# Group norm after a chunked scan: whole at the end, or chunk by chunk between the scan's own products

## The reference

```python
_, y = lax.scan(step, s0, (tm(rf), tm(decay), tm(kf), tm(vf), tm(kk), tm(af)))
y = tm(y)
mean = jnp.mean(y, axis=-1, keepdims=True)
var = jnp.mean(jnp.square(y - mean), axis=-1, keepdims=True)
y = ((y - mean) * lax.rsqrt(var + GN_EPS)).reshape(B, S, D) * ln_g + ln_b
bonus = jnp.sum(rf * kf * r_k, axis=-1, keepdims=True) * vf
out = (y + bonus.reshape(B, S, D)) * g.astype(jnp.float32)
return out.astype(h.dtype) @ w_o
...
sh1, sc1, gt1, sh2, sc2, gt2 = jnp.split(jax.nn.silu(c) @ ada_w[layer] + ada_b[layer], 6, axis=-1)
```

## Time and profile before

| | us |
|---|---|
| median of 3 runs (975.66 to 986.0) | 978.39 |
| the profiled execution | 980.12 |
| its span, first to last instruction | 978.3 |
| last matrix addition of the scan ends | 306.65 |
| first product of the output projection | 354.0 |
| PE / DVE / ACT / POOL busy | 856.2 / 660.2 / 418.4 / 112.1 |

### The profile page before, as it was taken

One profiled execution on the slowest core, in us unless ns is written; L12 is line 12 of the kernel. 1 busy time (PEld: TensorE's weight loads), 2 busy tenths in 40 slices (PEclk: granted clock), 3 DMA queues, 4 the chain that ended last, 5 costly groups with the idle time before them and its releaser, 6 DMA issues.

```text
span 978.3 us, 17529 instructions
## 1 busy us (share of the span) xinstructions
PE 856.2 (88%) x7477; PEld 733.1 (75%) x7477; DVE 660.2 (67%) x710; ACT 418.4 (43%) x585; POOL 112.1 (11%) x175
## 2 busy tenths in 40 slices
PE   1599997678888888999999999997777899999997
PEld 1597886567776455999999878995445689999976
DVE  4897965557557375999999957365675468545553
ACT  3279222333433146444343355514664653344441
POOL 8400002232331030000000003200000000000000
PEclk9799899799999689999999999996898999999999
DMA  8922335232205307799999556742000538655551
GB/s 322 338 89 85 100 116 197 76 118 88 89 13 189 129 20 258 259 372 368 368 370 384 201 172 208 213 140 77 1 1 1 173 129 278 238 175 194 192 172 43
DMA packets 71837, 170.16 MB, mean 174 GB/s; under 512 B 5432, under 2 KB 6736, under 8 KB 71760
## 3 DMA queue, kind: packets, MB, share of 16 engines
...
## 4 chain that ended last, share of the span: by engine, by line
PE 52%; DVE 34%; ACT 7%; issue 3%; DMA 2%; POOL 1%; ACTq 0%; DVEq 0%; POOLq 0%
DVE wlo L1025 8%; PE ps L1694 5%; PE ps L1698 5%; PE ps L1696 5%; PE ps L1683 5%; PE ps L1686 5%; PE ps L1685 5%; DVE acc L1269 5%; DVE acc L965 3%; PE ps L1620 2%; DVE gt L965 2%; PE ps L1512 2%; PE ps L1514 2%; PE ps L1515 2%; ACT whi L612 2%
## 5 line engine op out<-in xcount | busy, mean ns | idle before, releaser
L1025 DVE TENSOR_TENSOR wlo<-raw,whi 128x2048 fp32r<-128x2048 f32 x94 | 215.5, 2292 | 68.8 <-ACT whi L612 66.8
L612 ACT ACTIVATE whi<-raw 128x2048 fp32r<-128x2048 f32 x94 | 179.2, 1912 | 134.0 <-DMA raw<-in_mlp_down_dram 90.9
L1683 PE MATMUL ps<-ghi,whi 128*128 128x256 f32 x576 | 163.6, 284 | 2.5 <-DVE wlo L1025 1.4
L1686 PE MATMUL ps<-ghi,wlo 128*128 128x256 f32 x576 | 163.0, 283 | 0.0
L1685 PE MATMUL ps<-glo,whi 128*128 128x256 f32 x576 | 163.0, 283 | 0.0
L1683 PEld LDWEIGHTS ps<-ghi,whi 128*128 128x128 f32 x576 | 110.5, 192 | 5.1 <-issue 4.6
L1685 PEld LDWEIGHTS ps<-glo,whi 128*128 128x128 f32 x576 | 110.5, 192 | 0.7 <-issue 0.2
L1686 PEld LDWEIGHTS ps<-ghi,wlo 128*128 128x128 f32 x576 | 110.5, 192 | 0.0
L1694 PE MATMUL ps<-whi,hidhi 128*128 128x512 f32 x256 | 100.9, 394 | 2.4 <-DVE wlo L1025 2.4
L1696 PE MATMUL ps<-whi,hidlo 128*128 128x512 f32 x256 | 99.7, 390 | 0.0
L1698 PE MATMUL ps<-wlo,hidhi 128*128 128x512 f32 x256 | 99.6, 389 | 0.0
(11 more groups left out here) (337 smaller groups left out, 1637.7 us busy)
## 6 DMA issues: line engine op xcount, KB each, us to landing
raw<-in_mlp_up_dram SPq DMA_DIRECT2D x32, 1024.0 KB, 5.7
raw<-in_mlp_down_dram SPq DMA_DIRECT2D x32, 1024.0 KB, 5.2
raw<-in_ada_w_dram SPq DMA_DIRECT2D x24, 1024.0 KB, 6.1
late<-in_ada_w_dram SPq DMA_DIRECT2D x24, 1024.0 KB, 9.6
late<-in_kv_ada_w_dram SPq DMA_DIRECT2D x8, 1024.0 KB, 8.3
raw<-in_kv_w_dram SPq DMA_DIRECT2D x6, 1024.0 KB, 5.3
raw<-in_rw_k_dram SPq DMA_DIRECT2D x4, 1024.0 KB, 9.2
raw<-in_rw_r_dram SPq DMA_DIRECT2D x4, 1024.0 KB, 5.1
```

The costliest lines, as they stand in the source:

```text
L612: sc.activation(whi[i][:, :, :], raw[i][:, :].rearrange("p (k n) -> p k n", k=4), ACT.Copy).then_inc(s_hi, 1)
L1025: st.tell(dv.tensor_tensor(wlo[i][:, :, :], raw[i][:, :].rearrange("p (k n) -> p k n", k=4), whi[i][:, :, :].bitcast(F32), ALU.subtract), ...
L1683: mm(out_, whi[b][:, k, cols], hi[:, k0 + k, :], start=(first and k == 0 and m % 2 == 0), stop=False, skip_group_check=True)
L1686: ins = mm(out_, wlo[b][:, k, cols], hi[:, k0 + k, :], start=False, stop=False, skip_group_check=True)
```

## The change

The group norm is taken apart into entries of the scan's list, for 64 tokens each: `bonus` (spread the bonus sums, then on DVE times v, plus the norm's bias, times the gate, in place in `vF`), `centre` (one product with the matrix `centre`, identity minus head mean, gives the centred y; ACT squares it, DVE multiplies it by the gate times the norm's scale, `glng`), `variance` (head sums, root, reciprocal), `spread` (reciprocals back over features; DVE multiplies and adds), `high` and `low` (the split into `zhi`, `zlo`). Chunk c-1's stand inside chunk c. The list's ten places per chunk (after each `z` and each `p` pair) now hold several entries each, and `w`, `u`, `s`, `y`, `prep`, `turn`, `values` stand at other places. The four `rw_o` pieces are split in the last chunk (`piece_high`, `piece_low`). Behind the scan token block 0 of the projection is made in eight half pieces (`project`, 6 products each) between the last chunk's `u`, `y` and its norm; `out_projection` then makes token block 1 only. Modulation pieces 20 to 23 leave the place behind the scan: one stands behind the K/V pieces in the stream, three behind the query pieces, DVE does them there, and their column product is made on PE in the attention loop at unit 5. ACT makes `glng` ahead of the scan. `keep_clock(9)` goes.

```diff
+ADA_UNTIL = (6, 9, ADA_PIECES, ADA_PIECES)
...
-        between = [(x, c - 1, 0) for x in "wusy"] if c else []
...
+        slots = [[] for _ in range(10)]
+        if c == 0:
+            slots[0] = [("bonus", 0, 0)]
+            slots[7] = [("w", 0, 0)]
+        else:
+            slots[0] = [("u", before, 0)]
+            slots[1] = [("s", before, 0)]
+            slots[2] = [("y", before, 0)]
+            slots[7] = [("w", c, 0)]
+            if c >= 2:
+                slots[0].append(("high", c - 2, 0))
+                slots[1].append(("low", c - 2, 0))
         if c + 1 < NCH:
-            between += [(x, c + 1, h) for h in range(2) for x in ("prep", "turn")]
-            between += [("values", c + 1, 0)]
+            for n, x in enumerate((("prep", after, 0), ("turn", after, 0), ("prep", after, 1), ("turn", after, 1))):
+                slots[n + 3 if c else n + 1].append(x)
+            slots[7 if c else 5].insert(0, ("values", after, 0))
+            slots[9 if c else 8].append(("bonus", after, 0))
+            if c:
+                slots[4].append(("centre", before, 0))
+                slots[6].append(("variance", before, 0))
+                slots[8].append(("spread", before, 0))
+        else:
+            slots[3] = [("centre", before, 0), ("piece_high", 0, 0)]
+            slots[4] = [("piece_low", 0, 0), ("piece_high", 1, 0)]
+            slots[5] = [("variance", before, 0), ("piece_low", 1, 0), ("piece_high", 2, 0)]
+            slots[6] = [("piece_low", 2, 0), ("piece_high", 3, 0)]
+            slots[8] = [("spread", before, 0), ("piece_low", 3, 0)]
+            slots[9] = [("high", before, 0)]
...
                 order += [(x, c, 0, level), (x, c, 1, level)]
-                if between:
-                    order.append(between.pop(0))
+                order += slots[2 * level + i]
...
-    return order + [(x, NCH - 1, 0) for x in "wuy"]
...
+    return order + [("u", last, 0), ("low", last - 1, 0), ("project", 0, 0), ("y", last, 0), ("project", 1, 0),
+                    ("centre", last, 0), ("project", 2, 0), ("variance", last, 0), ("project", 3, 0), ("project", 4, 0),
+                    ("spread", last, 0), ("gate", 0, 0), ("high", last, 0), ("low", last, 0),
+                    ("project", 5, 0), ("project", 6, 0), ("project", 7, 0)]
...
-        scan_pieces = (ada_pieces(ada0, 3) + ada_pieces(ada0, 4) + ada_pieces(ada0, 2) + ada_pieces(ada1, 4)
-                       + square(A["rw_o"][0]))
+        scan_pieces = ada_pieces(ada0, 3) + ada_pieces(ada0, 4) + ada_pieces(ada0, 2) + square(A["rw_o"][0])
...
         place("kv", kv_pieces)
+        place("norm_a", ada_pieces(ada1, 4)[0:1])
         place("q", square(A["nsa_wqg"][0]))
+        place("norm_b", ada_pieces(ada1, 4)[1:4])
...
+            for j in range(KC):
+                sc.activation(glng[:, j, :], gF[:, j, :], ACT.Copy, scale=pt1[:, LNG + j:LNG + j + 1])
-            weight_high(12)
-            weight_high(13)
-            act.wait_ge(n_cent, 1)
-            sc.activation(sqF[:, :, :], yF[:, :, :], ACT.Square).then_inc(n_sq, 1)
-            act.wait_ge(n_var_ps, 1)
...
-            sc.activation(rs16[:, :], ps[0:H, 4, 0:S], ACT.Sqrt, scale=1.0 / N, bias=gnepsc[0:H, :]).then_inc(n_gstd, 1)
...
-            for h in range(2):
-                act.wait_ge(n_gn, h + 1)
-                for j in range(4 * h, 4 * h + 4):
-                    ins = sc.activation(yF[:, j, :], yF[:, j, :], ACT.Identity, scale=pt1[:, LNG + j:LNG + j + 1],
-                                        bias=pt1[:, LNB + j:LNB + j + 1])
-                ins.then_inc(n_aff, 1)
-            for h in range(2):
-                act.wait_ge(n_z, h + 1)
-                sc.activation(half_of(ghi, h), half_of(zF, h), ACT.Copy).then_inc(n_zhi, 1)
-            weight_high(14)
-            weight_high(15)
+                elif what == "centre":
+                    act.wait_ge(n_mean_ps, c + 1)
+                    sc.activation(sqc[:, :, :].rearrange("p j t -> p (j t)"), bank(7), ACT.Square).then_inc(n_sq, 1)
+                elif what == "variance":
+                    act.wait_ge(n_var_ps, c + 1)
+                    sc.activation(rs16[:, :], ps[0:H, 7, 0:N], ACT.Sqrt, scale=1.0 / N, bias=gnepsc[0:H, :]).then_inc(n_gstd, 1)
+                elif what == "high":
+                    act.wait_ge(n_z, c + 1)
+                    sc.activation(zhi[:, :, N * c:N * c + N], yF[:, :, N * c:N * c + N], ACT.Copy).then_inc(n_zhi, 1)
+                elif what == "piece_high":
+                    if c == 0:
+                        act.wait_ge(s_y_ps, NCH - 1)
+                    weight_high(12 + c)
+                elif what == "bonus":
+                    v.wait_ge(n_bb_ps, c + 1)
+                    vc = chunked(vF, c)
+                    st.tell(dv.tensor_tensor(vc, vc, eight(bank(5)), ALU.mult), T["bv"])
+                    st.do(dv.tensor_tensor(vc, vc, pt1[:, LNB:LNB + 8].unsqueeze(2).to_broadcast([P, KC, N]), ALU.add))
+                    st.do(dv.tensor_tensor(vc, vc, chunked(gF, c), ALU.mult))
+                elif what == "centre":
+                    v.wait_ge(n_sq, c + 1)
+                    st.tell(dv.tensor_tensor(chunked(yF, c), eight(bank(7)), chunked(glng, c), ALU.mult), T["cent"])
+                elif what == "variance":
+                    v.wait_ge(n_gstd, c + 1)
+                    st.tell(dv.reciprocal(rs16[:, :], rs16[:, :]), T["grstd"])
+                elif what == "spread":
+                    v.wait_ge(n_gb_ps, c + 1)
+                    st.do(dv.tensor_tensor(chunked(yF, c), chunked(yF, c), eight(bank(7)), ALU.mult))
+                    st.tell(dv.tensor_tensor(chunked(yF, c), chunked(yF, c), chunked(vF, c), ALU.add), T["z"])
+                elif what == "low":
+                    v.wait_ge(n_zhi, c + 1)
+                    st.tell(dv.tensor_tensor(chunked(zlo, c), chunked(yF, c), chunked(zhi, c).bitcast(F32), ALU.subtract),
+                            T["zlo"])
+                elif what == "piece_low":
+                    weight_low(12 + c)
+                elif what == "gate":
...
             modulated([0, 1], "gmB1", "shB1", qhi, qlo)
             for q in range(kv0 + 2, q0 + 2):
                 weight_low(q)
+                if q == kv0 + 4:
+                    v.wait_ge(n_acc5, 16 * 8)
+                    ada_piece(20, gt[1], 0, False)
...
             v.wait_ge(n_tanh, 1)
             st.do(dv.scalar_tensor_tensor(both(hc), both(hx), 1.0, both(hc), ALU.add, ALU.mult))
             st.tell(dv.tensor_scalar(both(hc), both(hc), 0.5, None, ALU.mult), T["hc"])
+            for i in range(1, 4):
+                ada_piece(20 + i, gt[1], i, False)
             v.wait_ge(n_hcT_ps, 1)
...
+                    biased_cols(column(6, 0), pt2[:, 48:56], V["gmB2"], 10)
...
-                        pe.wait_ge(s_y, c)
+                        pe.wait_ge(n_z, c)
...
+                elif what == "bonus":
+                    pe.wait_ge(s_bkt, 2 * c + 2)
+                    for j in range(KC):
+                        ins = mm(ps[:, 5, N * j:N * j + N], indt[:, P * j:P * j + P], s16[:, N * c:N * c + N], start=True, stop=True)
+                    ins.then_inc(n_bb_ps, 1)
+                elif what == "centre":
+                    pe.wait_ge(s_y, c + 1)
+                    mm(ps[:, 7, :], centre[:, :], yF[:, :, N * c:N * c + N], start=True, stop=True).then_inc(n_mean_ps, 1)
+                elif what == "variance":
+                    pe.wait_ge(n_cent, c + 1)
+                    for j in range(KC):
+                        ins = mm(ps[0:H, 7, 0:N], ind[:, j, :], sqc[:, j, :], start=(j == 0), stop=(j == KC - 1))
+                    ins.then_inc(n_var_ps, 1)
+                elif what == "spread":
+                    pe.wait_ge(n_grstd, c + 1)
+                    for j in range(KC):
+                        ins = mm(ps[:, 7, N * j:N * j + N], indt[:, P * j:P * j + P], rs16[:, :], start=True, stop=True)
+                    ins.then_inc(n_gb_ps, 1)
+                elif what == "gate":
+                    pe.wait_ge(n_bv, NCH)
+                    pe.wait_ge(s_v, NCH)
+                    pe.wait_ge(s_cols, 4)
+                    pe.wait_ge(s_ada, 8 + ADA_PIECES)
+                    gate_row(gt[0], 4)
+                elif what == "project":
+                    n, part = c // 2, c % 2
+                    ch, kh = n // 2, n % 2
+                    if c == 0:
+                        pe.wait_ge(s_zs[0], 5 * NCH)
+                        pe.wait_ge(s_zs[1], 5 * NCH)
+                        pe.wait_ge(n_zhi, TB)
+                        pe.wait_ge(n_zlo, TB)
+                    if part == 0:
+                        parts_ready(12 + n)
+                    ins = token_block(12 + n, 0, slice(0, 512), ps[:, ch, :], zhi, zlo, 4 * kh, kh == 0,
+                                      range(2 * part, 2 * part + 2))
+                    if c % 4 == 3:
+                        ins.then_inc(n_y, 1)
...
+                if not order:
```

(12 more changed lines are left out.)

197 lines of the change are left out of this document (76 added, 121 removed).

## The result

Over twenty runs each, the changed kernel takes 987.57 us (984.43 to 993.39) and the kernel before 978.49 (971.6 to 986.0): ratio 1.0101, 95% interval 1.008 to 1.0122. It is **slower by 1%**; I had forecast 968.2 with a range of 958 to 980. The profiled execution took 992.09 us with a span of 990.3, against 980.12 and 978.3 before, so the two traces lie 12.0 us apart.

A forecast was written before the change was run, and what follows sets the result against it. PE and DVE wait for each other in the scan, then a serial chain of 47.6 us precedes the projection. -40.1 + 27.1 + 2.8 - 2.0 + 1.1 + 0.9 = -10.2 us gives 968.2 from 978.39, range 958 to 980.

The forecast's parts named there:

- Part 1: Behind the scan: block 0 of the output projection ends 20 us after the scan instead of 60.1, minus 40.1 us.
- Part 2: Inside the scan: added norm and bonus entries and moved old ones lengthen the four chunks by 27.1 us, ends 18 and 36.
- the upper end of 36: Scan growth if all of DVE's added 27 us and half of PE's 17 are serial.
- its term: Forecast growth of each scan chunk, 0 to 3: +4.8, +6.7, +7.4 and +8.2 us.
- the expectation: Written for the old entries' order alone: places of `prep` and `w` cost 4 to 6 us, scan 146 to 148.
- the two pieces fewer: In chunk 3 of the scan, two modulation pieces fewer on DVE: -5.3 us.
- The clock: PE gaps lower its granted clock: three losses of 0.6 in the scan and 1.0 behind it, +2.8 us.
- the third rival: Gaps drop PE's clock in the scan to 0.75: 16 us on its path, 6 in the tail, 987; chance 0.07.
- Part 3: Four modulation pieces moved: first MLP's end -2.0, query stage +1.1, attention loop +0.9 us; ends -3 and +4.

The follow-up runs named there:

- before_new_order: The kernel before with only the changed kernel's places of the old entries, no norm, bonus or weight pieces in the scan: 990.1 us, ratio 1.0114.
- The small norm: The changed kernel with every norm and bonus entry kept in the scan but cut to 2 of 64 columns or times: 979.6 us, ratio 1.0007 to before.
- the one-weight bonus: The changed kernel with each bonus as one 512-column product instead of eight of 64, and `glng` made later: 979.4 us, ratio 1.0001 to before.
- the other order: The changed kernel with `prep` and `turn` of chunks 2 and 3 and `values` one place later, `centre`, `variance`, `spread` one earlier: 980.1 us, ratio 0.9971 to before.

## Why the prediction was wrong

It had the direction wrong: 968.2 forecast, 987.6 measured, outside the range. Point by point:

- **Part 1, the tail: right.** Block 0's last product ends 22.5 us behind the last `tt` addition (378.6 in the chain, against 356.1), 20 to 22 forecast, and PE has no gap of over 1 us there. Between the cuts of the table the gain is 37.7 of 39.1 forecast with the clock.
- **Part 2, the scan: the step that failed.** +40.7 where the sum had +27.1, beyond even the upper end of 36. Cut at PE's first products, every chunk is over its term, chunk 2 most: 7.5 for 4.8, 9.4 for 6.7, 13.9 for 7.4 and 9.9 for 8.2. Three things were mis-sized. First, "in proportion to 64 columns 1.0, I take 1.4" for `bonus` and `spread`: they measure 2.6 and 2.3, and still 2.0 with the clock at 0.98, since each of the eight products has its own weight load. PE pays 26.2 us in place of 17, of which 5.8 went away with the clock up. Second, the places of the old entries, which I had at some 4 to 6 us by the expectation, cost 8.3 with nothing added (before_new_order), a lower clock included. Third, the waits: I took it that part of the added work goes into idle time. DVE's added work was as forecast, 27.1 us, but its idle time did not shrink: it grew by 13.6, with 29.5 us of waits in front of `bonus` and `spread` and 24.1 fewer in front of `knr` and the narrow `tt`. The small norm took 5.8 us off the scan, the one-weight bonus 7.3, the other order 11.3. The weight pieces were 6.9 of chunk 3, where DVE's 9.2 us and the two pieces fewer had been set against each other.
- **The clock: under-sized.** I allowed +2.8. With the clock held up in both kernels the growth is 31.5 instead of 40.7, so 6 to 9 us are its share, most of it in chunk 0. The scan's mean fell from 0.92 to 0.83. This was the third rival's mechanism, and its 987 is what was measured, but by luck: it had 16 us for the clock on the scan's path and 6 in the tail, and the tail came out only 1.4 us short of the forecast. In my sum 9 in place of 2.8 would give some 974, still faster than before. Only with the rest of the scan's growth does the clock turn the sign: 31.5 of growth against 37.7 saved would be a gain, 40.7 is a loss. 0.07 was too little for a mechanism whose sign I had already seen in rows 1.
- **Part 3: right.** -0.9 from the second `pn` to `hcT`, made up as forecast, and +0.1 from there to the end of the kernel in all.
- **What the sum left out:** that the same instructions ahead of the scan can take up to 12.5 us more in one execution than in another. The traces' difference of 12.0 has 8.8 of it; sixteen starts give no reason to think that the measured difference of 9.1 comes from there, but the changed kernel itself started late three times in three, and 3 to 4 us stay open.

How the 40.7 us add up is not settled. The pieces measured one at a time (order 8.3, weight pieces 6.9, size of the norm's work 5.8, clock 6 to 9) overlap: the new order alone lowered the clock from 0.92 to 0.85, and the other order raised it from 0.83 to 0.88. What the exchanges cost by themselves, without PE's products, no run separates.
